# Chunk-wise norm behind the delta recurrence, leading parts first in the first tile, GpSimd held back, and sums of squares placed elsewhere, in a two-block network in one kernel

## The chip, the core and the metric

One core of a Trainium2 chip runs the whole program. The metric is the device time of one execution in microseconds (us). Engines are named as in the profile: PE is TensorE, PEld its weight loads, DVE VectorE, ACT ScalarE, POOL GpSimd, SP SyncE.

## The reference

512 tokens of width 1024, fp32. Two blocks follow each other. The first has a mixer of pooled means and a gated delta rule, then an MLP; the second has sparse attention and a state-space mixer. Here the first block matters, and of the second only its last product and norm.

```python
u = rms_norm(h, norm_mix[l])
proj = u @ w_in[l]                    # 20 tiles of 128 columns, and 8 columns a, b
...
def step(state, inp):                 # over chunks
    v_new = val - einsum(kc, state)
    o = einsum(qd, state) + einsum(ai, v_new)
    state = state * exp(gl) + einsum(kd, v_new)
...
o = o * lax.rsqrt(jnp.mean(o * o, axis=-1, keepdims=True) + EPS) * gdn_norm
o = o * jax.nn.silu(z)
...
h = h + mix @ w_out[l]                # mix: 512 pooled columns, then 4 heads of 128
u = rms_norm(h, norm_mlp[l])
h = h + jnp.square(jax.nn.relu(u @ w_up[l])) @ w_down[l]
```

## The kernel before

Activations lie transposed, 128 features per partition and 512 tokens along the row; hT holds x as eight such tiles (KT = 8). There is no scheduler: each engine has a list of instructions written out by hand, and they wait for each other by counting semaphores, so the order in the code is the order on the engine.

Each matrix product is made of three products of parts: a value is split into a leading part (suffix H, made by a rounding copy) and a rest (suffix L, the difference), and `product` (L396 to L398) adds leading x leading, rest x leading and leading x rest of one 128-row slice. The weights stream through a ring of four places (RING). One "half" is 128x512, four slices of one tile of outputs; two halves make a tile, so 24 products. SP loads half n into raw, POOL splits it (`split_weights`: a guard L1445, the cast L1446 into wh, the subtraction L1448 into wl; half_split counts), PE uses it (`half_slot`; half_used counts). A place of the ring is split again only when its half is used. Tiles alternate over four PSUM banks, and tile n+4 waits until tile n is evicted.

*The start.* ACT makes the leading parts of x times the norm weight (`weigh_lead`, L989, counted by g_lead) and DVE the rests (`weigh_rest`, L1539, counted by g_split); x comes in four pieces of two tiles. PE's first tile (`inp_tile(0)`) waits slice by slice for g_split. ACT then squares the eight tiles, DVE adds the squares (`add_square`, L1549), and `sum_squares(0)` (L389) sums them over the partitions by a product with ones, behind the second tile. `root` (L994, L995) makes the inverse root from it, which DVE needs for its first eviction (`evict_inp`, L1583). Behind tile 3 come the products with w_ab, whose small split POOL does between halves 3 and 4.

*The recurrence.* Four chunks of 128 tokens (NCH). Per chunk PE computes k x state (L649), the output of the chunk before (`scan_out`, L639 and L641) and the update (L661); DVE makes v_new and the state. ACT copies each chunk's output into gdnO (L1151). When all four are there ACT squares per head (L1155), PE sums (L668), ACT computes the inverse roots of four heads by Ln and Exp (`inverse_roots`, L970 and L973, with a table load before each), and DVE multiplies per head (L1749, L1752) into xs; ACT takes the leading part (`lead`, L1011) and DVE the rest (`rest`, L1534). `linear_apart("out")` takes the first four slices (the pooled ones) of tiles 0 to 3 first, 48 products, and their second halves after them; the first of these waits for m_split 5 to 8.

*The tail.* `linear_apart("sout")` is followed by residual additions (L1559), squares, additions, `sum_squares(4)`, the root, eight multiplications (L2210) and four output transfers of two tiles each (L1430).

## Time and profile before

| | us |
|---|---|
| median of 3 runs | 1330.87 |
| the runs | 1328.6, 1330.87, 1333.95 |
| profiled execution, its own time | 1328.44 |
| its span | 1326.6 |
| busy PE / POOL / DVE / ACT | 1271.9 / 857.1 / 779.4 / 414.0 |

The profiled execution's time holds 1.8 us around the span. Busy is the sum of what an engine's instructions took; what remains of PE's span, 54.7 us, is waiting. The mean granted clock of TensorE is 0.989 of full speed.

### The profile page before, as it was taken

Reading aid. Unit: us, or ns where it says so; the run is one execution under the profiler, and the core shown is the slowest. Engines: PE = TensorE matmul, PEld = TensorE weight load, DVE = VectorE, ACT = ScalarE, POOL = GpSimd, SP = SyncE. Lnnn points to the kernel's source line nnn. Section 1 sums busy time; section 2 is a strip of 40 time slices with the busy share of each in tenths; the row PEclk is TensorE's granted clock in tenths of the full one; section 3 lists DMA queues with packets and bytes.
Section 4 is the critical chain, followed back from the end, with each engine's and each line's share of the span. In section 5 each row is a group of like instructions: output and inputs, shape, how many; then the busy total and the mean of one; then the engine's idle time right before and its main releaser. Section 6 shows DMA issues by size and latency. Waiting matters only on the chain.

```text
span 1326.6 us, 21957 instructions
## 1 busy us (share of the span) xinstructions
PE 1271.9 (96%) x7696; PEld 1001.4 (75%) x7696; DVE 779.4 (59%) x1102; ACT 414.0 (31%) x850; POOL 857.1 (65%) x1078
## 2 busy tenths in 40 slices
PE   6999999899999999999999999899999999999995
PEld 4778897778877788888788798555557787878884
DVE  5968664689799211499438226277774659832223
ACT  4165744243301133211210021467773300331111
POOL 7767632777999777899778727312115875467772
PEclk9999999999999999999999999899999999999998
DMA  5222100253325433255495212100004459623331
GB/s 196 80 80 80 49 4 16 80 141 95 95 80 198 138 117 95 87 154 163 111 320 158 72 48 82 46 1 1 1 1 176 142 143 269 208 72 96 95 95 71
DMA packets 86476, 137.89 MB, mean 104 GB/s; under 512 B 16512, under 2 KB 34432, under 8 KB 85376
## 3 DMA queue, kind: packets, MB, share of 16 engines
q1 hardware_dynamic: 48384, 88.10, 22.2%
q10 hardware_dynamic: 38016, 48.71, 11.6%
q8 instruction: 55, 0.90, 0.3%
q14 instruction: 21, 0.17, 0.0%
HBM read 119.02 MB, written 20.91 MB: 105 GB/s over the span
## 4 chain that ended last, share of the span: by engine, by line
PE 82%; DVE 7%; issue 4%; POOL 3%; ACT 2%; DMA 1%; ACTq 1%; POOLq 0%; DVEq 0%
PE ps L396 20%; PE ps L398 20%; PE ps L397 20%; PE ps L811 3%; PE ps L791 3%; PE ps L835 3%; PE ps L549 2%; POOL small L1445 2%; DVE acc L1549 1%; PE ps L695 1%; PE ps L740 1%; PE ps L899 1%; POOL wh L1446 1%; PE ps L539 1%; DVE uL L1539 1%
## 5 line engine op out<-in xcount | busy, mean ns | idle before, releaser
L1448 POOL TENSOR_TENSOR wl<-raw,wh 128x512 fp32r<-128x512 f32 x336 | 498.6, 1484 | 26.9
L1445 POOL TENSOR_TENSOR small<-small 1x1 f32<-1x1 f32 x336 | 122.4, 364 | 261.8 <-PE ps L398 256.1
L396 PE MATMUL ps<-uH,wh 128*128 128x512 f32 x672 | 266.1, 396 | 11.1 <-DVE uL L1539 11.1
L397 PE MATMUL ps<-uL,wh 128*128 128x512 f32 x672 | 262.5, 391 | 0.0
L398 PE MATMUL ps<-uH,wl 128*128 128x512 f32 x672 | 262.3, 390 | 0.0
L1446 POOL CAST wh<-raw 128x512 fp32r<-128x512 f32 x336 | 203.3, 605 | 0.0
L396 PEld LDWEIGHTS ps<-uH,wh 128*128 128x128 f32 x672 | 126.6, 188 | 40.2 <-issue 11.0
L397 PEld LDWEIGHTS ps<-uL,wh 128*128 128x128 f32 x672 | 126.8, 189 | 27.2 <-issue 1.4
L398 PEld LDWEIGHTS ps<-uH,wl 128*128 128x128 f32 x672 | 126.7, 189 | 26.5
L396 PE MATMUL ps<-ffH,wh 128*128 128x512 f32 x256 | 101.4, 396 | 4.3 <-POOL wl L1448 4.3
L397 PE MATMUL ps<-ffL,wh 128*128 128x512 f32 x256 | 99.8, 390 | 0.0
L398 PE MATMUL ps<-ffH,wl 128*128 128x512 f32 x256 | 99.7, 390 | 0.0
L1511 POOL TENSOR_TENSOR bigA<-small 128x512 f32<-128x512 f32 x16 | 16.6, 1040 | 128.5 <-PE ps L844 100.0
L1313 ACT ACTIVATE bigB<-bigB,small 128x512 f32<-128x512 f32 (+3 forms) x128 | 70.3, 551 | 31.8 <-DVE small L2037 31.8
L2037 DVE CUSTOM_DVE_ANT_0 bigB<-ps,bigB 128x512 f32<-128x512 f32 (+3 forms) x128 | 57.3, 486 | 38.6 <-issue 23.5
L1559 DVE TENSOR_TENSOR hT<-hT,ps 128x512 f32<-128x512 f32 x40 | 27.5, 687 | 68.8 <-PE ps L398 68.3
L396 PEld LDWEIGHTS ps<-ffH,wh 128*128 128x128 f32 x256 | 48.0, 188 | 18.1 <-POOL wl L1448 6.1
L1889 DVE TENSOR_TENSOR ffL<-bigB,ffH 128x512 f32 x16 | 11.5, 719 | 79.4 <-ACT ffH L1231 79.4
L811 PEld LDWEIGHTS ps<-const_table,bigB 128*128 128x128 f32 x320 | 33.9, 141 | 31.9 <-issue 22.2
L1549 DVE TENSOR_TENSOR acc<-acc,xs 128x512 f32<-128x512 f32 x42 | 55.8, 1341 | 1.1 <-ACT xs L986 0.5
L398 PEld LDWEIGHTS ps<-ffH,wl 128*128 128x128 f32 x256 | 48.0, 188 | 10.2
L397 PEld LDWEIGHTS ps<-ffL,wh 128*128 128x128 f32 x256 | 48.1, 188 | 9.6
(395 smaller groups left out, 2395.0 us busy)
## 6 DMA issues: line engine op xcount, KB each, us to landing
raw<-wstream SPq DMA_DIRECT2D x336, 256.0 KB, 2.6
b_powers_scratch<-bigB ACTq DMA_DIRECT2D x4, 1024.0 KB, 5.1
c_powers_scratch<-bigB ACTq DMA_DIRECT2D x8, 512.0 KB, 4.1
lags_scratch<-lag_rows_scratch ACTq DMA_DIRECT2D x8, 512.0 KB, 8.4
bigB<-b_powers_scratch ACTq DMA_DIRECT2D x4, 1024.0 KB, 9.2
bigB<-lags_scratch ACTq DMA_DIRECT2D x4, 1024.0 KB, 6.6
bigB<-c_powers_scratch ACTq DMA_DIRECT2D x4, 1024.0 KB, 10.0
hT<-x ACTq DMA_DIRECT2D x4, 512.0 KB, 7.3
```

The costliest lines, as they stand in the source:

```text
L396: pe.matmul(out, lh, rh, start=first, stop=False)
L397: pe.matmul(out, lh, rl, start=False, stop=False)
L398: return pe.matmul(out, ll, rh, start=False, stop=last)
L791: i = pe.matmul(ps[:, u % 2 * 2 + half, 0:W], nsT[P, t, qt * 128:(qt + 1) * 128], nsT[P, 12 + 2 * b + t // 4, 0:W], start=True, stop=True)
L811: i = pe.transpose(ps[:, 4 + at // 512, at % 512:at % 512 + 128], prob[:, u % 6, half, kt * 128:(kt + 1) * 128], ident)
L835: i = pe.matmul(ps[64 * half:64 * half + 64, 7, kt * 128:512], vtok[:, kt, b * 256 + h * DH:b * 256 + (h + 1) * DH], probT[g % 2][:, half, ...
L1313: i = act.activation(prob[:, n % 6, half, 0:W], prob[:, n % 6, half, 0:W], ACT.Exp, scale=-1.0, bias=anmax[:, n % 3, half:half + 1], accum ...
L1445: pool.tensor_tensor(small[0:1, 569 + j:570 + j], zero_ap[0:1], zero_ap[0:1], ALU.add)
L1446: pool.tensor_copy(wh[:, j, :], raw[:, j, :]).then_inc(half_lead, 1)
L1448: pool.tensor_tensor(wl[:, j, :], raw[:, j, :], wh[:, j, :].bitcast(f32), ALU.subtract).then_inc(half_split, 1)
L1549: dve.tensor_tensor(acc[:, i, :], acc[:, i, :], xs[:, i if n == 2 else k % 2, :], ALU.add).then_inc(sq_added, 1)
L2037: i = dve.tensor_tensor_reduce(prob[:, u % 6, half, 0:W], ps[:, u % 2 * 2 + half, 0:W], dsl[t % 2][:, half, 512 - W:512], -1.0, 3e38, ALU. ...
```

## The change

It has these parts.

- **First tile** (`first_tile`): all 16 products that need only leading parts of x come first, two per slice as the part is ready, then the eight with the rests.
- **GpSimd held**: before it splits half 2 it waits for the sixth rest (`rests=KT - 2`); the second four halves now come ahead of w_ab. Before half 4 of "out" it waits for x_full, DVE's last step of the norm.
- **First sum** behind the third tile. ACT loads the table of Ln at its start.
- **Delta norm by chunks**: after each chunk's copy comes its square; the sum of chunk 0 stands within chunk 2, those of chunks 1 and 2 behind the recurrence, that of chunk 3 behind the first slice of "out". ACT makes the root of chunk 0 between chunks 1 and 2. DVE multiplies by chunks, in place; ACT makes four leading parts, DVE four rests.
- **Tail**: the last sum is two products, one of the first seven squares added up, one of the eighth. The output goes in five transfers.

```diff
@@ -189,6 +189,7 @@
+        go_bank = [4, 6, 5, 7]
@@ -355,7 +356,7 @@
-        SQUARES = [KT - 1, 2 * (KT - 1), 4 * (KT - 1), 5 * (KT - 1), 6 * (KT - 1)]
+        SQUARES = [KT - 1, 2 * (KT - 1), 4 * (KT - 1), 5 * (KT - 1), 6 * (KT - 1) - 1]
@@ -366,6 +367,12 @@
+        def go_squares(c):
+            return urr[1][:, c, :]
...
+        def of_chunk(x, c):
+            return x[:, 0:NHG, c * CH:(c + 1) * CH]
@@ -397,7 +404,7 @@
-            def half_slot(out, n, j, right, first, last, ready=None):
+            def half_slot(out, n, j, right, first, last, ready=None, between=None):
@@ -405,6 +412,8 @@
+                    if k == 0 and between is not None:
+                        between()
@@ -424,14 +433,14 @@
-            def linear_apart(name, x, ready):
+            def linear_apart(name, x, ready, between=None):
...
-                              h == 0, h == 1, (ready, 4 * h) if t == 0 else None)
+                              h == 0, h == 1, (ready, 4 * h) if t == 0 else None, between if i == 0 else None)
@@ -440,14 +449,29 @@
-                              lambda k: (uH[:, h * 4 + k, :], uL[:, h * 4 + k, :]), h == 0, h == 1,
-                              (g_split, 4 * h) if n == 0 else None)
...
-            inp_tile(0)
+                              lambda k: (uH[:, h * 4 + k, :], uL[:, h * 4 + k, :]), h == 0, h == 1)
...
+            def first_tile():
...
+                for h in range(2):
+                    pe.wait_ge(half_split, h + 1)
+                    for k in range(4):
+                        pe.wait_ge(g_lead, 4 * h + k + 1)
+                        for n, w in enumerate((wh, wl)):
+                            pe.matmul(ps[:, 0, :], w[:, h, k * 128:(k + 1) * 128], uH[:, h * 4 + k, :],
+                                      start=h == k == n == 0, stop=False)
+                for h in range(2):
+                    for k in range(4):
+                        pe.wait_ge(g_split, 4 * h + k + 1)
+                        i = pe.matmul(ps[:, 0, :], wh[:, h, k * 128:(k + 1) * 128], uL[:, h * 4 + k, :],
+                                      start=False, stop=h == 1 and k == 3)
+                    i.then_inc(half_used, 1)
...
+            first_tile()
...
+            inp_tile(2)
...
-            inp_tile(2)
@@ -641,6 +665,11 @@
+            def scan_squares(c):
...
+                pe.wait_ge(go_sq, c + 1)
+                pe.matmul(ps[:, go_bank[c], :], ones, go_squares(c), start=True, stop=True).then_inc(go_sum, 1)
@@ -649,6 +678,8 @@
+                    if c == 2:
+                        scan_squares(0)
@@ -662,13 +693,10 @@
-            for h in range(NHG):
-                pe.wait_ge(go_sq, h + 1)
-                pe.matmul(ps[:, 4 + h, :], ones, urr[1].rearrange("p a b -> p (a b)")[:, h * T:(h + 1) * T],
-                          start=True, stop=True).then_inc(go_sum, 1)
+            for c in range(1, NCH - 1):
+                scan_squares(c)
...
-            linear_apart("out", (mH, mL), m_split)
+            linear_apart("out", (mH, mL), m_split, between=lambda: scan_squares(NCH - 1))
@@ -942,7 +970,10 @@
-            sum_squares(4)
+            pe.wait_ge(sq_added, SQUARES[4])
+            pe.matmul(ps[:, 4, :], ones, acc[:, 0, :], start=True, stop=False)
+            pe.wait_ge(sq_done, SQUARED[4] + KT)
+            pe.matmul(ps[:, 4, :], ones, xs[:, (KT - 1) % 2, :], start=False, stop=True).then_inc(rms_sum, 1)
@@ -961,6 +992,7 @@
+            act.preload_act_table_set("natural_log")
@@ -1145,18 +1177,23 @@
+            def scan_roots(chunks):
+                inverse_roots(chunks, lambda c: of_chunk(qkvT, c), lambda c: ps[:, go_bank[c], :].rearrange("p (h c) -> p h c", c=CH),
+                              1.0 / 128, lambda c: act.wait_ge(go_sum, c + 1), go_std)
...
-                act.activation(gdnO[:, :, c * CH:(c + 1) * CH], src, ACT.Copy).then_inc(sc_oe, 1)
-            act.wait_ge(sc_oe, NCH)
-            sq = urr[1].rearrange("p a b -> p (a b)")
+                act.activation(of_chunk(gdnO, c), src, ACT.Copy).then_inc(sc_oe, 1)
+                act.wait_ge(sc_oe, c + 1)
+                act.activation(go_squares(c).rearrange("p (h c) -> p h c", c=CH), of_chunk(gdnO, c), ACT.Square).then_inc(go_sq, 1)
+                if c == 1:
+                    scan_roots(range(0, 1))
+            scan_roots(range(1, NCH))
+            act.wait_ge(x_full, NHG)
...
-                act.activation(sq[:, h * T:(h + 1) * T], gdnO[:, h, :], ACT.Square).then_inc(go_sq, 1)
-            inverse_roots(range(NHG), lambda h: qkvT[:, h, :], lambda h: ps[:, 4 + h, :], 1.0 / 128,
-                          lambda h: act.wait_ge(go_sum, h + 1), go_std)
-            for h in range(NHG):
-                lead(mH[:, 4 + h, :])
+                act.activation(mH[:, 4 + h, :], gdnO[:, h, :], ACT.Copy).then_inc(x_lead, 1)
+            full[0] = NHG
@@ -1425,19 +1462,22 @@
-            for k in range(0, KT, 2):
-                act.wait_ge(rms_out, k + 2)
-                act.dma_start(out_dram[:, k:k + 2, :], hT[:, k:k + 2, :]).then_inc(out_done, 16)
-            act.wait_ge(out_done, KT // 2 * 16)
+            parts = ((0, 2), (2, 4), (4, 6), (6, 7), (7, 8))
+            for lo, hi in parts:
+                act.wait_ge(rms_out, hi)
+                act.dma_start(out_dram[:, lo:hi, :], hT[:, lo:hi, :]).then_inc(out_done, 16)
+            act.wait_ge(out_done, len(parts) * 16)
...
-            def split_weights(lo, hi):
+            def split_weights(lo, hi, rests=None):
...
+                        if rests is not None and j == 2:
+                            pool.wait_ge(g_split, rests)
@@ -1461,9 +1501,10 @@
-            split_weights(0, RING)
+            split_weights(0, RING, rests=KT - 2)
+            split_weights(RING, 2 * RING)
...
-            split_weights(RING, 2 * SLOT0["out"] + RING)
+            split_weights(2 * RING, 2 * SLOT0["out"] + RING)
@@ -1486,6 +1527,7 @@
+            pool.wait_ge(x_full, NHG)
@@ -1742,19 +1784,18 @@
-            dve.wait_ge(sc_o, NCH)
...
+            for c in range(NCH):
+                dve.wait_ge(go_std, c + 1)
+                own(dve.scalar_tensor_tensor(of_chunk(gdnO, c), of_chunk(gdnO, c), param("gdn_norm"), of_chunk(qkvT, c), ALU.mult, ALU.mult))
+                i = dve.tensor_tensor(of_chunk(gdnO, c), of_chunk(gdnO, c), projT[:, 16:20, PAD + c * CH:PAD + (c + 1) * CH], ALU.mult)
+            i.then_inc(x_full, NHG)
+            dve.wait_ge(m_split, 4)
...
-                dve.wait_ge(go_std, h + 1)
-                own(dve.scalar_tensor_tensor(gdnO[:, h, :], gdnO[:, h, :], param("gdn_norm"), qkvT[:, h, :], ALU.mult, ALU.mult))
-                if h >= 2:
-                    dve.wait_ge(m_split, 4 + h - 1)
-                dve.tensor_tensor(xs[:, h % 2, :], gdnO[:, h, :], projT[:, 16 + h, PAD:PW], ALU.mult).then_inc(x_full, 1)
-                if h >= 1:
-                    if h == 1:
-                        dve.wait_ge(m_split, 4)
-                    rest(mL[:, 3 + h, :], mH[:, 3 + h, :]).then_inc(m_split, 1)
-            rest(mL[:, 7, :], mH[:, 7, :]).then_inc(m_split, 1)
+                dve.wait_ge(x_lead, h + 1)
+                dve.tensor_tensor(mL[:, 4 + h, :], gdnO[:, h, :], mH[:, 4 + h, :].bitcast(f32), ALU.subtract).then_inc(m_split, 1)
+            split[0] = NHG
@@ -2203,7 +2244,12 @@
-            residual("sout", 4, lambda k: add_square(4, k) if k else None)
+            for k in range(KT - 1):
+                add_tile("sout", k)
+                if k > 1:
+                    add_square(4, k - 1)
+            add_square(4, KT - 2)
+            add_tile("sout", KT - 1)
```

The start, on PE: the first rows before (names: uH and uL are leading part and rest of x, wh and wl those of the weights).

```order
L396 MATMUL ps<-uH,wh 128x512 [waits weighted_split,half_split]
L397 MATMUL ps<-uL,wh 128x512
L398 MATMUL ps<-uH,wl 128x512
L396 MATMUL ps<-uH,wh 128x512 [waits weighted_split]
L397 MATMUL ps<-uL,wh 128x512
L398 MATMUL ps<-uH,wl 128x512
```

And with the change, the first rows and those around the end of the first tile's leading products:

```order
L461 MATMUL ps<-uH,wh 128x512 [waits weighted_lead,half_split]
L461 MATMUL ps<-uH,wl 128x512
L461 MATMUL ps<-uH,wh 128x512 [waits weighted_lead]
L461 MATMUL ps<-uH,wl 128x512
...
L461 MATMUL ps<-uH,wh 128x512 [waits weighted_lead]
L461 MATMUL ps<-uH,wl 128x512
L466 MATMUL ps<-uL,wh 128x512 [waits weighted_split] x8
L403 MATMUL ps<-uH,wh 128x512 [waits half_split]
L404 MATMUL ps<-uL,wh 128x512
```

Each slice's product with uL has gone behind the 16 others. On POOL, around half 2, with the change:

```order
L1485 TENSOR_TENSOR small<-small 1x1 [waits half1_loaded]
L1486 CAST wh<-raw 128x512
L1488 TENSOR_TENSOR wl<-raw,wh 128x512 [waits half_lead]
L1485 TENSOR_TENSOR small<-small 1x1 [waits weighted_split,half2_loaded]
L1486 CAST wh<-raw 128x512
L1488 TENSOR_TENSOR wl<-raw,wh 128x512 [waits half_lead]
```

The guard of half 2 waits for weighted_split (g_split). On PE, between the end of the recurrence and "out", before (uT is the squares, mH and mL the mixed activations):

```order
L639 MATMUL ps<-bigA,mixT 128x128
L641 MATMUL ps<-bigB,mixT 128x128
L668 MATMUL ps<-uT,const_table 128x512 [waits gdn_squares] x4
L396 MATMUL ps<-mH,wh 128x512 [waits half_split,mixed_split,tile_evicted,scan_state]
L397 MATMUL ps<-mL,wh 128x512
L398 MATMUL ps<-mH,wl 128x512
L396 MATMUL ps<-mH,wh 128x512 [waits mixed_split]
L397 MATMUL ps<-mL,wh 128x512
L398 MATMUL ps<-mH,wl 128x512
```

With the change:

```order
L663 MATMUL ps<-bigA,mixT 128x128
L665 MATMUL ps<-bigB,mixT 128x128
L671 MATMUL ps<-uT,const_table 128x512 [waits gdn_squares] x2
L403 MATMUL ps<-mH,wh 128x512 [waits half_split,mixed_split,tile_evicted,scan_state]
L404 MATMUL ps<-mL,wh 128x512
L405 MATMUL ps<-mH,wl 128x512
L671 MATMUL ps<-uT,const_table 128x512 [waits gdn_squares]
L403 MATMUL ps<-mH,wh 128x512 [waits mixed_split]
L404 MATMUL ps<-mL,wh 128x512
L405 MATMUL ps<-mH,wl 128x512
L403 MATMUL ps<-mH,wh 128x512 [waits mixed_split]
```

Of the four sums two stand there and one behind the first three products; the fourth is earlier. On ACT, from the first copy of a chunk, before:

```order
L1151 ACTIVATE uT<-ps 128x4x128 [waits scan_out] x4
L1155 ACTIVATE uT<-uT 128x512 [waits scan_out_copied]
L1155 ACTIVATE uT<-uT 128x512 x3
L970 ACT_TABLE_LOAD
L970 ACTIVATE bigA<-ps,small 128x512 [waits gdn_sum] x4
L973 ACT_TABLE_LOAD
L973 ACTIVATE bigA<-bigA 128x512 [waits act_chain]
L973 ACTIVATE bigA<-bigA 128x512 x3
L1011 ACTIVATE mH<-xs 128x512 [waits x_full] x4
```

With the change:

```order
L1187 ACTIVATE uT<-ps 128x4x128 [waits scan_out]
L1189 ACTIVATE uT<-uT 128x512 [waits scan_out_copied]
L1187 ACTIVATE uT<-ps 128x4x128 [waits scan_out]
L1189 ACTIVATE uT<-uT 128x512 [waits scan_out_copied]
L1002 ACT_TABLE_LOAD
L1002 ACTIVATE bigA<-ps,small 128x4x128 [waits gdn_sum]
L1005 ACT_TABLE_LOAD
L1005 ACTIVATE bigA<-bigA 128x4x128 [waits act_chain]
L1187 ACTIVATE uT<-ps 128x4x128 [waits scan_out]
L1189 ACTIVATE uT<-uT 128x512 [waits scan_out_copied]
L1187 ACTIVATE uT<-ps 128x4x128 [waits scan_out]
L1189 ACTIVATE uT<-uT 128x512 [waits scan_out_copied]
```

Squares follow the copies, and two table loads have come in between the second and the third chunk.

## Rows read from the trace of the kernel before

**Rows 1.** The page, busy time and share of the span by engine.

```profile
PE 1271.9 (96%) x7696; PEld 1001.4 (75%) x7696; DVE 779.4 (59%) x1102; ACT 414.0 (31%) x850; POOL 857.1 (65%) x1078
```

**Rows 2.** Timeline, start to 31 us: start us, length, engine line what [idle<-releaser].

```profile
6.15 1.28 ACT L989 ACT_TABLE_LOAD   x1 [6.15 <-DMA hT<-x]
...
8.20 8.46 DVE L1539 SCALAR_TENSOR_TENSOR uL<-hT,param_table,uH 128x512 fp32r<-128x512 f32 x8 [3.38 <-ACT uH L989]
...
9.56 0.76 PE L396 MATMUL ps<-uH,wh 128*128 128x512 f32 x1 [9.56 <-DVE uL L1539]
...
11.61 1.33 ACT L989 ACTIVATE uH<-hT,param_table 128x512 fp32r<-128x512 f32 x2 [0.31 <-DMA hT<-x]
...
14.58 0.63 PE L397 MATMUL ps<-uL,wh 128*128 128x512 f32 x1
...
15.01 0.43 PE L398 MATMUL ps<-uH,wl 128*128 128x512 f32 x1
...
21.76 0.64 POOL L1445 TENSOR_TENSOR small<-small 1x1 f32<-1x1 f32 x1
...
23.26 0.39 PE L398 MATMUL ps<-uH,wl 128*128 128x512 f32 x1
...
24.58 0.64 POOL L1445 TENSOR_TENSOR small<-small 1x1 f32<-1x1 f32 x1
...
26.46 1.10 PE L389 MATMUL ps<-acc,const_table 128*128 128x512 f32 x2 [2.82 <-DVE acc L1549]
...
30.94 0.63 ACT L995 ACTIVATE rms<-rms 128x512 f32<-128x512 f32 x1
```

**Rows 3.** Timelines, 215 to 241 us; a window: engines' busy time, granted clock last but two.

```profile
215.09 0.60 ACT L1151 ACTIVATE uT<-ps 128x512 f32<-128x512 f32 x1 [1.19 <-PE ps L641]
...
216.40 3.70 PE L668 MATMUL ps<-uT,const_table 128*128 128x512 f32 x8 [1.35 <-ACT uT L1155]
...
217.92 1.28 ACT L970 ACT_TABLE_LOAD   x1
...
219.22 2.43 ACT L970 ACTIVATE bigA<-ps,small 128x512 f32<-128x512 f32 x4
...
222.93 0.18 POOL L1445 TENSOR_TENSOR small<-small 1x1 f32<-1x1 f32 x1 [25.87 <-PE ps L398]
...
229.07 1.22 DVE L1534 TENSOR_TENSOR mL<-xs,mH 128x512 fp32r<-128x512 f32 x1
...
233.06 1.75 DVE L1534 TENSOR_TENSOR mL<-xs,mH 128x512 fp32r<-128x512 f32 x1
...
219.53 0.80 PE L396 MATMUL ps<-mH,wh 128*128 128x512 f32 x1
...
234.87 0.50 PE L396 MATMUL ps<-mH,wh 128*128 128x512 f32 x1 [3.19 <-DVE mL L1534]
...
240.38 0.40 PE L398 MATMUL ps<-mH,wl 128*128 128x512 f32 x1
...
236.80:240.40 3.60, 3.54 (x9) 2.78 (x10) 1.33 (x3) 0.07 (x1) 0.58 (x2) 0.53 0.02 5
```

**Rows 4.** Timelines of ScalarE and VectorE, tail; window with DMA share last but one.

```profile
1313.18 1.28 ACT L994 ACT_TABLE_LOAD   x1
1315.47 0.69 ACT L994 ACTIVATE rms<-ps,small 128x512 f32<-128x512 f32 x1 [1.01 <-PE ps L389]
...
1313.56 0.69 DVE L1549 TENSOR_TENSOR acc<-acc,xs 128x512 f32<-128x512 f32 x1 [0.46 <-ACT xs L986]
...
1323.00:1325.00 2.00, 0.00 (x0) 0.00 (x0) 0.53 (x1) 0.00 (x0) 0.00 (x0) 0.50 0.99 395
```

**Rows 5.** VectorE's first rests, 0 to 20 us: count, min/median/max ns.

```profile
L1539 DVE SCALAR_TENSOR_TENSOR uL<-hT,param_table,uH x8: 740/1010/1772, 8.2 to 15.8; 128x512 fp32r<-128x512 f32 x8
```

**Rows 6.** Timeline of VectorE near 75 us.

```profile
75.29 0.69 DVE L1583 TENSOR_TENSOR bigA<-ps,rms 128x512 f32<-128x512 f32 x1 [4.52 <-PE ps L398]
```

**Rows 7.** Waits of TensorE, 355 to 436 us: total, times, longest us.

```profile
PE ps L396 <- POOL wl L1448: 4.3, 5, 1.0
```

## The prediction

> **What bounds the kernel now.** I read the page first: TensorE is busy 96% of the span [rows 1], so only time in which it waits, or runs at its lower clock, can be won. The table of what TensorE waited for, narrowed to each stage, gives the places, and the order of instructions in time shows them one by one. Three of them lie where the change works.
>
> - *The start.* The first product is at 9.56, though a split weight half is there much earlier. It waits for VectorE's first rest (uL), which waits for ScalarE's first leading part, which waits for a table load that only begins when x has landed. Then the first tile's products come at a pace of 0.43 us each until 15.01, and at 0.229 us from there on (36 products from 15.01 to 23.26). From 23.49 to 26.46 TensorE stands before the first sum of squares, because VectorE's eight rests and seven additions are not through [rows 2].
> - *The end of the chunk recurrence.* ScalarE copies the last chunk at 215.09, squares four heads, TensorE sums them from 216.40, ScalarE changes tables twice, VectorE multiplies. TensorE covers this with 48 products of "out" and then stands still, 3.19 us at 234.87; the tile that waits is finished at 240.61 (its last product starts at 240.38) [rows 3].
> - *The tail.* Last addition, sum, root, output: nothing runs beside it [rows 4].
>
> VectorE is slow beside GpSimd when its inputs lie in SBUF: the eight first rests take 0.74 to 1.77 us [rows 5], two rests of "out" 1.22 and 1.75 [rows 3], while an addition at 1313.56, with GpSimd idle, takes 0.69 [rows 4]. That is what "GpSimd held back" buys.
>
> **The start, step by step.** All times are in the clock of the old trace. The table is loaded before x lands, so leading part 1 is ready at 6.15 + 0.70 = 6.9 instead of 8.2. The first tile now runs its 16 products that need only leading parts, two per part. ScalarE makes the parts at 0.64 us each; the last two wait for the fourth piece of x at 11.61 [rows 2] and end at 12.95, so the table load saves nothing there. The 16 products end at 12.95 + 2 x 0.43 = 13.8. VectorE's rests, 0.74 us each with GpSimd idle [rows 5], keep step: the sixth at about 11.9, the eighth at 13.7. Eight products are left: 1.8 us at the faster pace. It came 5.4 us after the first product before; the same here would be 12.3, so I take it. The tile ends at 15.6; before, at 18.05 (the second tile's 24 products end at 23.49). If the pace is still the slow one it is 8 x 0.43 = 3.4, and 17.2.
>
> GpSimd's hold goes on until the sixth rest, 11.9. Its steps per half (guard, cast, subtraction) took 24.58 - 21.76 = 2.82 us beside VectorE [rows 2]; so halves 2 to 7 end at 14.7, 17.6, 20.4, 23.2, 26.0 and 28.8. TensorE wants halves 2 to 5 at 15.6, 18.3, 21.1 and 23.8, and after the sum (0.94) halves 6 and 7 at 27.5 and 30.2. The smallest margin is 0.6 us, so the hold costs nothing; if it lasts 1 us longer it costs 0.4. The small split of w_ab, now behind half 7, ends at 30, and is wanted at 33. The sum of squares stands behind the third tile at 26.5; the additions end before 24, so the wait of 2.97 us goes. **Gain: 2.45 + 2.97 = 5.4 us**, 5.2 with a trifle for GpSimd's margin; bounds 3.4 (the slow pace, 3.8, and a hold 1 us longer) and 6.0 (the last piece of x 0.6 us sooner). What is late next: the inverse root, ready at 31.57 before, comes at about 30.3 (sum at 26.5, no table load before Ln), and VectorE then works off a backlog without a pause until 70.8. Its first wait for TensorE after that, up to 75.29, was 4.52 us [rows 6], so with 1.3 us from the earlier root it can follow a shift of 5.8. That just covers 5.2.
>
> **The recurrence.** TensorE gets the same four sums (0.86 us each, four in 3.70 us at 216.40 [rows 3]) at other places. The first goes into chunk 2 ahead of the output of chunk 1 and delays what follows by 0.86, as VectorE was already done there. The outputs of the last chunk end at 215.7 instead of 214.9. ScalarE now makes a copy and a square of 0.6 us per chunk, and between chunks 1 and 2 the root of chunk 0: two table loads of 1.28 us [rows 3] and two activations, from 211.2 to 215.1. So the last copy and square, one behind the other with chunk 2's, end at 217.5, against 217.9 for four squares. Sums 1 and 2 are done at 217.5, "out" begins there (219.53 before) and takes sum 3 in behind its third product; its first 48 products end at 229.3. ScalarE: load to 218.8, three Ln, the last after sum 3, to 220.6, load, Exp at 222.5, 223.1 and 223.6. VectorE: two steps per chunk of 0.74 + 0.69 us, since GpSimd is held, so x_full at 222.5 + 3 x 1.45 = 226.8. Before, most of the same steps ran beside GpSimd's splitting. Then four leading parts at 0.55 to 0.63 us and four rests; GpSimd starts its splits at 226.8 too (222.93 before [rows 3]), so the rests take between 0.7 and 1.75 us; I take 1.4, from the two measured there, 1.22 and 1.75 [rows 3]. They end at 229.1, 230.5, 231.9 and 233.3. Half 4 of the weights is split at 229.4. The waiting tile ends at 233.3 + 0.7 = 234.0; before, 240.61. The later halves, one per 2.82 us from 229.4, stay ahead of TensorE, which wants them at 234.0, 236.7 and 239.4 (half 7 by 237.9). **Gain 6.6 us.** Bounds: 8.3 with rests of 0.7 us, 5.0 with the clock below. I take 6.2.
>
> The load of a table shows as 1.28 us, and the Ln behind it starts at once, at 219.22, so I price each of the two added loads at that [rows 3].
>
> **The tail.** The last square ends at 1313.17, the last addition starts 0.39 us later, takes 0.69, and the sum starts at 1314.31. Now the sum of the first seven squares is taken at once behind the last tile, and the last square is its own second product, from 1313.2 to 1314.3. The Ln then starts at 1314.5, as its table load ends at 1314.46 [rows 4]: 1.0 us before the old 1315.47. The last output is issued in smaller pieces, but the transfer engines are 99% busy from 1323 to 1325 [rows 4], so this gives 0 to 0.4; I take 0. **Gain 1.0 us**, bounds 0.8 and 1.4.
>
> **The sum**: 5.2 + 6.2 + 1.0 = 12.4 us. From the profiled execution's 1328.44 that is 1316.0; the median of the runs shown is 2.4 us above that execution, so I forecast **1318.5 us**. Between the three places TensorE is the chain nearly everywhere, and waits for work that itself follows TensorE, so the gains should be carried to the end.
>
> **Rivals.**
> *The clock takes a share back.* In the window from 236.8 to 240.4 the granted clock is 0.53, the lower level but for its end, and nine products take 3.6 us, after TensorE had waited twice [rows 3]. The new kernel waits there as well, between single groups of three products, about 2.5 us in all, and in the first tile its products come in pairs with gaps. If the clock is at 1.2 GHz through the first tile's last eight products (1.6 us) and again through eight of "out" (1.6 us), the gain is 9.2: 1321.7. For it: that window. Against it: the new waits are shorter. The page "TensorE: Matmul & The Clock Gate" of the Trainium skill, What's actually happening, says that the array is at half rate by default and that activity releases it; the trace agrees, with the slow pace up to 15.01. Chance 0.2.
> *A change of tables costs more than its load.* The detour to chunk 0's root holds ScalarE from 211.2 to 215.1, and each us longer comes one for one out of "out". If each of the two loads in it cost as much again as it shows, 2.6 us, the time is 1321.1. Against it: the step from the load at 217.92 to the next activation is 1.30 us [rows 3]. Chance 0.05. The Trainium skill, "ScalarE: Activation LUTs", What ACT_TABLE_LOAD costs, says so: a drain of about 1.38 us comes with every load, 2.66 us in all. By that page the detour is 2.8 us longer and the sum 9.6; the trace shows no such drain.
> *The start's gain is lost on the way.* Stretches that hang on GpSimd exist: around the first "up" and "down" TensorE waited five times for a split, 4.3 us [rows 7]. If such a stretch, or VectorE's backlog before 70.8, doesn't move forward with TensorE, the 5.2 is gone and 1323.7 remains. For it: VectorE's margin is only 0.6 us. Against it: in every one of these stretches GpSimd itself begins on TensorE's release. Chance 0.12.
> *The holds make GpSimd the bound: slower.* Both holds delay the splits, and TensorE pays one for one beyond its margin: 0.6 us at the start, 0 to 4 in "out". It turns the result from where the two holds together last 13 us longer than I have them (the 12.4 and the margin); at 15.6 us, the loss is 15 against the forecast: 1333.5. For it: before the change the eight rests lasted until 16.66. Against it: they did so beside GpSimd. Chance 0.03.
> *It doesn't do what it says*: the rests stay slow with GpSimd idle, or x's pieces land later. Then the start gives 3 and "out" 3, and 1323.9 results. Chance 0.05.
> The forecast's own case has 0.55.
>
> **How the numbers follow.** About 0.5%, 6.7 us, is what a measurement of this kernel can tell from no change. The forecast, the clock rival and the table rival, 0.8 together, lie beyond it; of the other two, 7.2 and 7.0 us are just beyond, so I count half of their 0.17 as faster, and take off a little for the spread of the runs (5.35 us between three of them): faster 0.85, same 0.12, slower 0.03. Range: upper bounds of all terms, 6.0 + 8.3 + 1.4 = 15.7, and 2.3 us of spread give 1313; the lost start, with 1.8 us of spread, gives 1325.5.
>
> **What would show it.** Right: first product near 7; first tile done by 16; no wait before the first sum; rests of 0.75 us there; "out" beginning near 217.5 less the shift of 5, its waiting tile done 6 to 7 us earlier relative to the last recurrence step; Ln of the tail 1.0 us sooner. Wrong: a TensorE wait for wl of halves 2 to 7 or 4 of "out", the low clock in the first tile or behind the waits of "out", or VectorE idle no more near 75 and TensorE waiting for its small gate step (L494).

## The result, and the profile after

| | before | changed |
|---|---|---|
| median, us | 1331.01 (4 runs, 1328.6 to 1333.95) | 1321.64 (4 runs, 1321.18 to 1323.33) |
| ratio | | 0.9927, 95% interval 0.9914 to 0.994 |
| profiled execution, its own time | 1328.44 | 1323.33 |
| its span | 1326.6 | 1321.5 |

The change is 9.4 us faster: the side that was forecast, 3.1 us short of the forecast time of 1318.5, inside the range. The two profiled executions differ by only 5.1 us. Before's was the fastest of its runs and the changed kernel's the slowest, so where the time went is read from places, not from the spans. Of all runs told of below, one took 1609.95 us (x5, granted clock 0.747); the ratios leave it out.

**A ruler.** GpSimd makes one subtraction (wl) for each of the 336 weight halves, in the same order in every version. The start of the n-th in a trace, taken from the start of the n-th in the trace of before, says by how much a version is ahead at that place. Halves are counted from 0. Hereafter "lead at half n" is that difference, positive when the version is ahead. For the changed kernel:

```
half   12    20    24    28    40  |  60    188 |  192   232 |  244   300 | end of the span
lead   5.3   5.0   2.4   1.9   1.9 |  7.7   7.8 |  6.1   6.0 |  4.2   4.2 | 5.1
```

It makes 5 us at the start, loses 3 between halves 20 and 28, makes 5.9 at the recurrence, loses 1.7 and 1.8 in two stretches at the lower clock in the middle (3.4 us long from 651.8, where before has none, and 17.1 us long from 849.8, where before has 13.7), and makes 0.9 at the tail.

The page, busy time by engine, answers to [rows 1]: TensorE has 3.8 us more busy time in a span 5.1 us shorter. Busy time holds the products at the lower clock, so it is no measure of work.

```profile
PE 1275.7 (97%) x7698; PEld 1002.5 (76%) x7698; DVE 773.1 (59%) x1101; ACT 415.7 (31%) x851; POOL 856.8 (65%) x1078
```

**The start**, the timeline of the changed kernel to 31 us, by engine (start us, length, engine, line, what, idle time before and who ended it), answers to [rows 2]:

```profile
4.82 1.28 ACT L995 ACT_TABLE_LOAD   x1 [4.82 <-issue]
...
8.16 1.34 ACT L1021 ACTIVATE uH<-hT,param_table 128x512 fp32r<-128x512 f32 x2 [0.70 <-DMA hT<-x]
...
6.99 0.77 PE L461 MATMUL ps<-uH,wh 128*128 128x512 f32 x1 [6.99 <-ACT uH L1021]
7.55 0.63 PE L461 MATMUL ps<-uH,wl 128*128 128x512 f32 x1
7.98 0.63 PE L461 MATMUL ps<-uH,wh 128*128 128x512 f32 x1
...
9.96 0.47 PE L461 MATMUL ps<-uH,wh 128*128 128x512 f32 x1
10.27 0.40 PE L461 MATMUL ps<-uH,wl 128*128 128x512 f32 x1
...
13.68 2.28 PE L466 MATMUL ps<-uL,wh 128*128 128x512 f32 x8
15.80 0.39 PE L403 MATMUL ps<-uH,wh 128*128 128x512 f32 x1
...
26.71 1.02 PE L396 MATMUL ps<-acc,const_table 128*128 128x512 f32 x2
...
6.88 3.81 DVE L1581 SCALAR_TENSOR_TENSOR uL<-hT,param_table,uH 128x512 fp32r<-128x512 f32 x4 [2.09 <-ACT uH L1021]
...
12.47 2.93 DVE L1581 SCALAR_TENSOR_TENSOR uL<-hT,param_table,uH 128x512 fp32r<-128x512 f32 x2 [0.20 <-ACT uH L1021]
...
30.64 0.69 DVE L1625 TENSOR_TENSOR bigA<-ps,rms 128x512 f32<-128x512 f32 x1 [5.53 <-PE ps L405]
...
12.43 0.18 POOL L1485 TENSOR_TENSOR small<-small 1x1 f32<-1x1 f32 x1 [4.28 <-DVE uL L1581]
```

The first product is at 6.99 (9.56 before). ScalarE makes the leading parts as x lands, and waits for it three times, at 8.16 for 0.70 us. TensorE reaches its faster pace at about 9.96: the step to the next product is 0.31 us there, against 0.43 from 7.55 to 7.98. Seven of the eight rest products follow each other at 0.23 us, the eighth starts at 15.46, when its rest is there; the tile ends at 15.80, and the first sum, at 26.71, has no idle time ahead of it. VectorE's rests, merged in these rows, take 1.82 us for the first, beside GpSimd's split of half 1, 0.74 to 0.75 for each of the next five, with GpSimd held, and 1.23 and 1.78 for the last two, once GpSimd is released at 12.43.

**The gate step**, the same view from 62 to 78 us, VectorE, ScalarE and TensorE:

```profile
63.56 0.68 DVE L1625 TENSOR_TENSOR bigA<-ps,rms 128x512 f32<-128x512 f32 x1
...
69.21 2.81 DVE L1658 SCALAR_TENSOR_TENSOR bigA<-bigA,param_table 128x512 f32<-128x512 f32 x3 [2.14 <-ACT bigA L1064]
71.95 0.68 DVE L1625 TENSOR_TENSOR bigA<-ps,rms 128x512 f32<-128x512 f32 x1
...
77.23 0.18 DVE L1687 SCALAR_TENSOR_TENSOR small<-small 128x16 f32<-128x16 f32 x1
...
63.67 0.22 ACT L1086 ACTIVATE small<-small 128x16 f32<-128x16 f32 x1 [5.29 <-DVE small L1677]
...
68.47 0.71 ACT L1064 ACTIVATE bigA<-bigA,param_table 128x512 f32<-128x512 f32 x1
...
75.25 0.39 PE L405 MATMUL ps<-uH,wl 128*128 128x512 f32 x1
77.46 0.39 PE L518 MATMUL ps<-small,const_table 128*128 128x16 f32 x2 [1.82 <-DVE small L1687]
```

VectorE takes 32.9 us from its first eviction (30.64) to that of tile 6 (63.56); before, it took 30.3 (31.76 to 62.03). Here are the two rows of before that answer to 63.56 and 69.21, with the first product behind the recurrence's waiting tile, which is needed further down:

```profile
239.53 0.63 PE L396 MATMUL ps<-mH,wh 128*128 128x512 f32 x1
...
62.03 0.68 DVE L1583 TENSOR_TENSOR bigA<-ps,rms 128x512 f32<-128x512 f32 x1
...
67.68 3.09 DVE L1616 SCALAR_TENSOR_TENSOR bigA<-bigA,param_table 128x512 f32<-128x512 f32 x3 [0.38 <-ACT bigA L1032]
```

So tile 6's eviction comes 1.5 us later than before, though everything up to there began 1.1 us earlier. A chain hangs on VectorE's step right before that eviction (L1677): four activations of ScalarE from 63.67, with three table loads between them, then its scaling at 68.47, then VectorE's next block at 69.21, which is 1.5 us later than before too. VectorE's work then ends at 71.95, where before it ended at 70.77 and stood idle for 4.52 [rows 6]. The gate step (L1687) is ready at 77.41, and TensorE, whose last product started at 75.25, waits 1.82 us for it. Then the clock falls. Windows of TensorE there (length, busy time, granted clock, DMA share, GB/s):

```profile
78.00:80.00 2.00, 2.00 (x7) 0.60 0.24 86
80.00:82.00 2.00, 2.00 (x7) 0.55 0.30 103
```

**The recurrence**, timeline from 205 to 233 us, answers to [rows 3]:

```profile
215.17 0.80 PE L403 MATMUL ps<-mH,wh 128*128 128x512 f32 x1
...
227.86 0.50 PE L403 MATMUL ps<-mH,wh 128*128 128x512 f32 x1 [0.36 <-POOL wl L1488]
...
231.25 0.50 PE L403 MATMUL ps<-mH,wh 128*128 128x512 f32 x1 [0.72 <-DVE mL L1796]
...
209.38 1.28 ACT L1002 ACT_TABLE_LOAD   x1
210.68 0.69 ACT L1002 ACTIVATE bigA<-ps,small 128x512 f32<-128x512 f32 x1
...
215.62 1.28 ACT L1002 ACT_TABLE_LOAD   x1
216.91 1.85 ACT L1002 ACTIVATE bigA<-ps,small 128x512 f32<-128x512 f32 x3
...
224.37 0.69 DVE L1791 TENSOR_TENSOR uT<-uT,bigA 128x512 f32<-128x512 f32 x1
225.83 5.36 DVE L1796 TENSOR_TENSOR mL<-uT,mH 128x512 fp32r<-128x512 f32 x4 [0.77 <-ACT mH L1195]
...
225.38 0.18 POOL L1485 TENSOR_TENSOR small<-small 1x1 f32<-1x1 f32 x1 [30.20 <-DVE uT L1791]
```

The root of chunk 0 lies between the chunks (209.38 to 213.31), "out" begins at 215.17, x_full is done at 225.06, the four rests take 1.34 us each, and the waiting tile is finished at 232.05. Where TensorE had waited 3.19 and 1.03 us and run at 0.53 of the clock [rows 3], it now waits 0.36 (for GpSimd's split of half 4 of "out", which the hold delays) and 0.72, and the clock stays at 1.00.

**The tail**, timeline, answers to [rows 4]:

```profile
1309.06 1.13 PE L976 MATMUL ps<-xs,const_table 128*128 128x512 f32 x2 [0.58 <-ACT xs L1018]
...
1308.38 0.63 ACT L1018 ACTIVATE xs<-hT 128x512 f32<-128x512 f32 x1 [4.81 <-DVE hT L1601]
1309.03 1.28 ACT L1026 ACT_TABLE_LOAD   x1
1310.32 0.69 ACT L1026 ACTIVATE rms<-ps,small 128x512 f32<-128x512 f32 x1
```

The product of the last square ends at 1310.19, ScalarE's table load at 1310.31, and Ln starts at once. From the start of the last square to the end of the span: 1308.38 to 1321.5, 13.1 us, against 14.07 before (1312.53 to 1326.6).

### The profile page after: what moved, and what is told of

It is laid out like the page before. It is cut to its first block, busy times and chain, and to the rows that moved or that the text cites. A ratio compares the mean times of both kernels' runs of the same rounds, so it can differ in the third digit from the quotient of the medians.

```text
span 1321.5 us, 21957 instructions
## 1 busy us (share of the span) xinstructions
PE 1275.7 (97%) x7698; PEld 1002.5 (76%) x7698; DVE 773.1 (59%) x1101; ACT 415.7 (31%) x851; POOL 856.8 (65%) x1078
## 4 chain that ended last, share of the span: by engine, by line
PE 80%; DVE 8%; issue 4%; POOL 3%; ACT 2%; DMA 1%; ACTq 1%; POOLq 0%; DVEq 0%
PE ps L403 20%; PE ps L404 19%; PE ps L405 19%; PE ps L839 3%; PE ps L819 3%; PE ps L863 3%; PE ps L573 2%; POOL small L1485 2%; PE ps L723 1%; PE ps L768 1%; PE ps L927 1%; POOL wh L1486 1%; PE ps L563 1%; DVE bigB L1632 1%; DVE bigA L2096 1%
## 5 line engine op out<-in xcount | busy, mean ns | idle before, releaser
L1485 POOL TENSOR_TENSOR small<-small 1x1 f32<-1x1 f32 x336 | 125.2, 373 | 258.1 <-PE ps L405 217.5
L403 PE MATMUL ps<-uH,wh 128*128 128x512 f32 x664 | 262.8, 396 | 1.5 <-DVE uL L1581 1.5
L404 PE MATMUL ps<-uL,wh 128*128 128x512 f32 x664 | 259.2, 390 | 0.0
L405 PE MATMUL ps<-uH,wl 128*128 128x512 f32 x664 | 259.2, 390 | 0.0
L1930 DVE TENSOR_TENSOR ffL<-bigB,ffH 128x512 f32 x16 | 11.1, 692 | 79.9 <-ACT ffH L1268 79.9
L819 PE MATMUL ps<-bigA 64*128 64x512 f32 (+3 forms) x256 | 54.8, 508 | 1.1 <-ACT bigB L1331 0.7
## 6 DMA issues: line engine op xcount, KB each, us to landing
bigB<-c_powers_scratch ACTq DMA_DIRECT2D x4, 1024.0 KB, 10.1
```

The source lines that it names most:

```text
L403: pe.matmul(out, lh, rh, start=first, stop=False)
L404: pe.matmul(out, lh, rl, start=False, stop=False)
L405: return pe.matmul(out, ll, rh, start=False, stop=last)
L819: i = pe.matmul(ps[:, u % 2 * 2 + half, 0:W], nsT[P, t, qt * 128:(qt + 1) * 128], nsT[P, 12 + 2 * b + t // 4, 0:W], start=True, stop=True)
L1485: pool.tensor_tensor(small[0:1, 569 + j:570 + j], zero_ap[0:1], zero_ap[0:1], ALU.add)
```

## The experiments

Twelve kernels. Medians beside the runs of before on the same chip (median 1331.1 of 19 runs for the first four, 1331.7 of 27 for the next, 1330.8 of 21 for the last). The change was measured beside its own four runs of before, so a difference of under 1 us between its median and another's is no finding. Leads are from each one's trace, one per kernel, by the ruler above.

| | median us | ratio, 95% | lead 12 | lead 20 | lead 28 | lead 60 | made at "out" |
|---|---|---|---|---|---|---|---|
| the change | 1321.6 | 0.991-0.994 | 5.3 | 5.0 | 1.9 | 7.7 | 5.86 |
| x1 start only | 1326.5 | 0.996-1.000 | 4.9 | 4.7 | 3.2 | 2.7 | |
| x2 recurrence only | 1322.9 | 0.992-0.996 | -1.8 | -1.7 | -1.7 | 4.1 | 5.84 |
| x3 tail only | 1330.3 | 0.998-1.000 | -2.2 | -1.7 | -1.7 | -2.0 | |
| x4 late gate | 1317.9 | 0.988-0.992 | 4.9 | 4.7 | 5.3 | 11.1 | 5.86 |
| x5 first sum late only | 1328.5 | 0.997-1.000 | 3.0 | 2.6 | 2.4 | 1.9 | |
| x6 no hold at "out" | 1325.2 | 0.994-0.998 | 4.8 | 4.7 | 3.1 | 5.7 | 2.54 |
| x7 no hold at the start | 1322.6 | 0.991-0.995 | 0.8 | 0.5 | 0.9 | 6.8 | 5.88 |
| x8 roots together | 1321.8 | 0.991-0.995 | 4.9 | 4.7 | 1.5 | 5.7 | 4.12 |
| x9 late gate, old start | 1331.3 | 0.999-1.001 | -2.0 | -1.6 | -1.1 | -1.7 | |
| x10 no early table load | 1322.2 | 0.990-0.994 | 3.8 | 3.6 | 0.4 | 6.3 | 5.87 |
| x11 tail, sum only | 1330.7 | 0.998-1.002 | -1.9 | -1.9 | -1.8 | -1.7 | |
| x12 late gate again | 1316.9 | 0.988-0.991 | 5.0 | 4.8 | 5.3 | 11.2 | 5.88 |

**One group of parts at a time** (x1 to x3). The edits are the parts of the change named in the section on it; x1 has `first_tile`, the late first sum, the early table load and the hold at the start; x2 the norm by chunks and the hold at "out"; x3 the last sum in two products and the five transfers.

```diff
-            inp_tile(0)
+            first_tile()
...
+            act.preload_act_table_set("natural_log")
...
+            split_weights(0, RING, rests=KT - 2)
```

> The start's parts alone in the old kernel (first tile's order, first hold of GpSimd, w_ab behind half 7, first sum behind the third tile, table of Ln at the start). Theory A (the gain is made and then lost to VectorE's backlog): the splits of halves 12 to 20 are 5.3 us earlier than in the old kernel, TensorE waits about 1.8 us at its small gate products near 77 us, then works through about ten products at the lower clock, and from half 28 on the lead is 1.9 us; the time is 1.9 us lower than before (1329), unclear within the noise. Rival B (the loss of 3.4 us comes from the other parts or was chance of one execution): no such wait and a time 5.3 us lower, 1325.7.

Lead 4.9 at half 12, 3.2 at half 28: 1.5 to 1.8 us are lost at the gate step, where TensorE waits 1.82 us as in the changed kernel. The clock did not fall behind that wait here, which is the rest of the difference to the changed kernel's 1.9. The median, 1326.5, is 2.5 us below theory A's 1329 and nearer to rival B's 1325.7. Theory A holds in the trace all the same, wait and loss are there; its 1.9 us were a lead over a trace of before that is faster than the usual one (see x2), and counted in a fall of the clock that didn't come.

```diff
+            for c in range(1, NCH - 1):
+                scan_squares(c)
...
+            linear_apart("out", (mH, mL), m_split, between=lambda: scan_squares(NCH - 1))
...
+            pool.wait_ge(x_full, NHG)
```

> The parts of the recurrence alone in the old kernel (norm by chunks, sums placed elsewhere, GpSimd held until x_full). Theory A: the chain through out's waiting tile is its own, so the splits from half 64 on are 5.9 us earlier than before and the time is 5.9 us lower, 1325. Rival B (it only gains because the start came earlier): under 3 us.

5.84 us made at "out". The lead is -1.7 up to there although nothing ahead of it was changed: with the old start, TensorE stands 2.37 us before the first sum and then runs at the lower clock. So does x3, so do x9 and x11 (3.2 to 3.3 us); only the trace of before doesn't, after 2.82 us. Before's profiled execution is a lucky one by 1.7 us. The median is 8.2 us below before's, where 5.9 was expected; the interval goes from 5.7 to 10.1. A part of the surplus is in the trace: its low stretch near 850 is 10.2 us long, 3.4 shorter than before's, and the lead grows there from 4.2 to 5.4.

```diff
-            sum_squares(4)
+            pe.wait_ge(sq_added, SQUARES[4])
+            pe.matmul(ps[:, 4, :], ones, acc[:, 0, :], start=True, stop=False)
...
+            parts = ((0, 2), (2, 4), (4, 6), (6, 7), (7, 8))
```

> The last sum in two products and five output transfers alone in the old kernel. Theory A: from the last square's start to the end 13.1 us instead of 14.1, time 1.0 us lower, within the noise of the runs; all of it before the Ln, none in the transfers. Rival B (smaller last transfers also end sooner): 1.3 us or more, and the end 2.7 us or less behind the last multiplication, 3.1 before.

Last square to the end 1314.83 to 1328.0, 13.2 us. The median is only 0.8 us below before, within what the runs can tell; the trace has it. The three medians add up to 13.7 us and the whole change made 9.4. With intervals as wide as x1's (0.4 to 5.6) and x2's, the runs don't tell whether the parts lose something together.

**The gate step moved** (x4), with the whole change in:

```diff
+            inp_tile(10)
             pe.wait_ge(gate_b, 2)
             pe.wait_ge(pool_out, 3)
             pe.matmul(ps[:, 6, 0:16], const("cumsum"), gg, start=True, stop=True)
             pe.matmul(ps[:, 6, 16:32], ones, gg, start=True, stop=True).then_inc(gate_mm, 1)
-            inp_tile(10)
```

> The changed kernel with TensorE's two small gate products (cumsum, sum of gg) moved from in front of tile 10 to behind it; VectorE reads them only after it has evicted tile 10. Theory A: TensorE no longer waits 1.8 us for VectorE's gate step there, does not fall to the lower clock behind it, and the lead over the old kernel stays 5.3 us from half 20 to half 40: time 3.4 us below the changed kernel, 1318.3. Rival B (VectorE is behind by then in any case and its next eviction or the sums of q and k wait instead): the wait shows up at the next place within 15 us and less than 1 us is won. Rival C (the clock falls at that place whatever TensorE waits for): 1.8 us is won and the low clock stays.

The windows of TensorE (columns as above) where the changed kernel had stood and then run at 0.60:

```profile
78.00:80.00 2.00, 2.00 (x10) 1.00 0.29 113
```

No wait, full clock, and the lead stays at 5.3 where the changed kernel falls to 1.9. One line moved is worth 3.4 us in the trace and about 4 in the medians.

**Is VectorE's backlog a fixed length?** (x5, from the kernel before)

```diff
             inp_tile(1)
-            pe.wait_ge(s_const, 16)
-            sum_squares(0)
             inp_tile(2)
+            pe.wait_ge(s_const, 16)
+            sum_squares(0)
```

> The kernel before with one edit: the product of the first sum of squares stands behind the third tile instead of behind the second. Theory A (VectorE's backlog from the root of that sum to the gate step is the second bound of the first 80 us): TensorE's wait ahead of the sum (2.4 to 3.3 us in the traces with the old start) goes and the clock stays high behind it, so the split of half 12 comes 3 us earlier than in the trace of before and 4.7 us earlier than in the two other traces with the old start; but the sum, and with it the root, comes 1 to 2 us later than at 30.94, so VectorE reaches the gate step 1 to 2 us later than before and TensorE waits there for 4 to 5 us: nothing is left of it by half 28, and the time is 1330 to 1332. Theory B (the lead is kept, and the wait at the gate step is small): half 28 and all after it 3 us or more earlier, time 1326.5 to 1328.5.

A miss for theory A as it was put. Timeline rows of TensorE at the gate step and of VectorE's evictions of tiles 0 and 6:

```profile
78.54 0.40 PE L494 MATMUL ps<-small,const_table 128*128 128x16 f32 x2 [0.97 <-DVE small L1645]
...
34.09 0.69 DVE L1583 TENSOR_TENSOR bigA<-ps,rms 128x512 f32<-128x512 f32 x1 [7.37 <-ACT rms L995]
...
62.97 0.68 DVE L1583 TENSOR_TENSOR bigA<-ps,rms 128x512 f32<-128x512 f32 x1
```

The root is 2.3 us later (33.90 against 31.57), but tile 6 is evicted only 0.9 us later: the stretch takes 28.9 us, where it took 30.3 before and 32.9 in the changed kernel. It isn't a fixed amount of work in time; VectorE's operations on SBUF take longer beside a GpSimd split (in the changed kernel the same multiplication, L1658, takes 0.74 to 1.65 us), and the earlier the stretch begins, the more splits not yet held up by TensorE lie beside it. The traces bear this out. Between the two evictions VectorE has the same 36 operations in all 14. GpSimd starts 8 subtractions (wl) there in x5, and the stretch takes 28.9 us; 9 in the kernel before, x2, x3, x7, x9 and x11, 29.8 to 30.8 us; 10 in x10, 31.6; 11 in the changed kernel, x1, x4, x6, x8 and x12, 32.9 to 33.0. That is about 1.3 us for a split more. No run changes the number of splits there by itself. TensorE's products of the gate step start at 78.54 here, at 77.77 in x1, 77.46 in the changed kernel and 78.94 in x10, although the roots of these lie up to 3.4 us apart. By itself this one edit keeps 2.4 of its 3 us by the ruler (more against the other traces with the old start, which lie at -1.7), and the time, 1328.5, is theory B's.

**The holds** (x6, x7).

```diff
-            pool.wait_ge(x_full, NHG)
```

> The changed kernel without GpSimd's wait for x_full ahead of the splits of the output projection's ring. Theory A (the hold buys short operations of VectorE, as taken in the prediction): the first split of that stretch starts at about 217 instead of 225.4, the multiplications of the last chunks take 0.8 to 1.3 us each instead of 0.69 to 0.75, x_full comes 1.5 to 3 us later than 225.06, the four remainders take 1.7 us each instead of 1.34, and the waiting tile ends 2.5 to 4.5 us later than at 232.05: time 1323.5 to 1326. Rival (the holds change nothing, since TensorE then waits for GpSimd instead): the tile ends within 0.5 us of 232.05 and the time is that of the changed kernel, 1321.6.

2.54 us made at "out" instead of 5.86: the hold is worth 3.3. The rows (VectorE's multiplications and rests, TensorE's wait):

```profile
225.65 1.58 DVE L1790 TENSOR_TENSOR uT<-uT,bigA 128x512 f32<-128x512 f32 x1
228.00 3.53 DVE L1795 TENSOR_TENSOR mL<-uT,mH 128x512 fp32r<-128x512 f32 x4 [0.77 <-ACT mH L1195]
...
229.87 0.47 PE L403 MATMUL ps<-mH,wh 128*128 128x512 f32 x1 [3.62 <-DVE mL L1795]
```

Five of the six multiplications take 1.2 to 1.7 us, more than the expected 0.8 to 1.3. Of the rests only the first takes 1.7 us; the other three take 0.68, not 1.7: GpSimd's fourth split ends at 229.2, the ring is full and GpSimd is quiet. x_full is ready at 227.24, and x6 is 1.2 us further ahead than the changed kernel up to there, so it is 3.4 us late, more than the 1.5 to 3 expected. TensorE stands 3.62 us, and the clock falls. The 3.3 us include what that fall costs.

```diff
-            split_weights(0, RING, rests=KT - 2)
+            split_weights(0, RING)
```

> The changed kernel without the hold at the start: GpSimd splits the third half as soon as it is there, beside VectorE's remainders. Theory A: the remainders take 1.2 to 1.8 us each instead of 0.94 to 1.46 and the last one ends at 16 to 17 instead of at 15.4, so the first tile ends 0.5 to 1.5 us later than at 15.80, and the splits from half 12 on come later by as much; since VectorE's backlog takes back what the start gains beyond the gate step anyway, the time stays within 0.7 us of 1321.6. Rival (the remainders are late because of the leading parts' arrival and not because of GpSimd): tile 0 ends at 15.8 as before, GpSimd is up to 4 us further ahead, and the stretch to the gate step is shorter, time 1320 to 1321.

```profile
7.25 11.02 DVE L1581 SCALAR_TENSOR_TENSOR uL<-hT,param_table,uH 128x512 fp32r<-128x512 f32 x8 [2.05 <-ACT uH L1021]
...
18.32 0.74 PE L466 MATMUL ps<-uL,wh 128*128 128x512 f32 x1 [1.17 <-DVE uL L1581]
18.87 0.63 PE L403 MATMUL ps<-uH,wh 128*128 128x512 f32 x1
```

The eight rests take 11.02 us, 1.38 each. TensorE waits 0.65 and 1.17 us within the first tile, which ends at 18.87, 3.1 us later than with the hold, more than theory A's 0.5 to 1.5, and the last rest ends at 18.27, where 16 to 17 was expected. The clock falls at 18.4 for 3.4 us, and the pace of 0.43 us follows. Lead 0.8 at half 12. Most of it doesn't matter, since at half 28 the changed kernel has only 1.9 left: 1.0 us in the trace and 0.9 in the medians, where at most 0.7 was expected.

**The root of chunk 0** (x8) and **the early table load** (x10), each taken out of the changed kernel:

```diff
-                if c == 1:
-                    scan_roots(range(0, 1))
-            scan_roots(range(1, NCH))
+            scan_roots(range(NCH))
```

> The changed kernel with the root of the first chunk not taken on its own but together with the other three: two table loads fewer on ScalarE, four chunks of logarithms and exponentials behind the last sum instead of three, and VectorE multiplies all four chunks behind it. Theory A (behind the last sum every operation on ScalarE and VectorE is on the path): the first exponential ends 0.6 us later and one more chunk of 1.4 us stands on VectorE, of which 0.3 to 0.7 us is given back since ScalarE's copy of chunk 2 no longer waits behind the root; x_full at 226.3 to 226.8 instead of 225.06, the waiting tile ends 1.2 to 1.7 us later, time 1322.8 to 1323.3. Rival (the two loads saved are worth as much as the chunk): x_full within 0.4 us of 225.06, time 1321.6.

```profile
220.70 2.20 ACT L1005 ACTIVATE bigA<-bigA 128x512 f32<-128x512 f32 x4
...
226.46 0.69 DVE L1789 TENSOR_TENSOR uT<-uT,bigA 128x512 f32<-128x512 f32 x1
...
229.93 0.80 PE L403 MATMUL ps<-mH,wh 128*128 128x512 f32 x1 [2.09 <-POOL wl L1486]
```

The exponentials end at 222.9 and x_full is ready at 227.15, 1.75 us later than in the changed kernel once its lead is the same (x8 is 0.34 us behind there). TensorE stands 2.09 us for GpSimd's split, which the hold ties to x_full, the clock falls behind that, and 4.12 instead of 5.86 us are made at "out". So two table loads more are the cheaper way in the trace, and the rival's "x_full within 0.4 us" is out. In the medians nothing of it shows: 1321.8 is the rival's time, 1 us below what was expected. Medians of 4 and of 10 runs that spread over several us don't resolve it, and x8's trace has a low stretch near 850 of 10.2 us, 6.8 shorter than the changed kernel's.

```diff
-            act.preload_act_table_set("natural_log")
```

> The changed kernel without the early load of the logarithm table. Theory A (the start's gain comes from the sum moved and from the order of the products, and the leading parts are paced by the arrival of x): the first leading part starts at 7.5 to 7.8 instead of at 6.12, the last one at most 0.5 us later than before (12.4), tile 0 ends 0 to 0.7 us later than at 15.80, and the table is loaded once before the first logarithm, at 28 to 30, which puts the root 1.3 us later; TensorE's wait at the gate step then grows by 0 to 1 us: time 1321.5 to 1322.8. Rival (each step of the start counts in full): tile 0 ends 1.3 us later and the time is 1323 to 1324.

A miss for theory A's steps, though the median, 1322.2, is in its range: the first tile ends at 17.34, 1.54 us later, and lead 28 is 0.4 against 1.9. The leading parts were nearly on time (the last at 13.5, against 13.06), but the first product comes at 8.90 instead of 6.99, and the pace stays at 0.43 us for 14 of the 16 products, against six in the changed kernel. What the early load buys here is an earlier start of TensorE's slow products, not earlier parts. How much of the 1.54 us that is, one trace doesn't tell. The faster pace came 6.1 us after the first product here. In the six traces with the new start and the hold (the change, x1, x4, x6, x8, x12) it came 3.0 to 5.3 us after it, and the tile ended at 15.62 to 16.16 wherever it came. Had it come 5.3 us after it here, products 13 to 24 would have run at 0.23 us and the tile ended near 16.9, 1.1 us late, by estimate from these rows; and after 4.3 us the tile would be 0.7 late.

**Two controls** (x9: x4's edit in the kernel before; x11: x3 with the four equal transfers) **and a repeat** (x12: x4 once more).

> The kernel before with one edit: the two products of the gate step stand behind the eleventh tile (tile 10) instead of behind tile 9. Theory A (at the gate step the old start leaves TensorE only 0 to 0.3 us early, so there is nothing to free): the wait of 0.25 us at those products goes, all splits behind half 24 stay within 0.4 us of the shift that they had at half 20, time that of before, 1331 to 1332. Rival (the gate products are better off later for another reason, by the order of the work on the other engines): 1 us or more faster than before.

Ratio 0.9998. In the lead, 0.5 us are won at the gate step (the wait of 0.25 and the products around it), 0.1 more than expected. What is worth 3.4 us behind the new start is worth next to nothing with the old one.

> The kernel before with the last sum of squares in two products (and the last addition on VectorE behind it), but with the four equal transfers at the end. Theory A (the sum carries all of the tail's gain, the last multiplication's end to the program's end was 3.08 us with four transfers and 3.13 with five): from the last square's start to the end 13.1 us, as in the changed kernel, against 14.07 before; time 1329.8 to 1330.7. Rival (the smaller last transfer carries half of it): 13.5 us or more from the last square to the end, time 1330.7 to 1331.2.

```profile
1315.77 0.63 ACT L989 ACTIVATE xs<-hT 128x512 f32<-128x512 f32 x1 [4.81 <-DVE hT L1562]
...
1317.71 0.69 ACT L997 ACTIVATE rms<-ps,small 128x512 f32<-128x512 f32 x1
```

Last square to the end of the span (1328.9): 13.1 us. The sum gives all of it, the fifth transfer nothing.

> The changed kernel with the gate step's products behind tile 10, a second time and in more runs, since its first median rests on four. Theory A (TensorE keeps the 5.3 us of the start instead of 1.9 to 3.2): splits 28 to 40 stand 5.0 to 5.5 us ahead of before, and the median lies 2 to 4 us below the changed kernel's 1321.6, at 1317.5 to 1319.5. Rival (the first result was a lucky set of runs, and the clock takes the lead back elsewhere): 1320 to 1322.

1316.9, ratio 0.9896. Over both, nine runs lie between 1316.1 and 1319.6, the changed kernel's four between 1321.2 and 1323.3. This version beats both kernels.

**Where the clock fell.** From short windows of granted clock over all 14 traces. A fall is to 0.50, the lower of the two levels:

| TensorE had stood | traces | clock fell behind it |
|---|---|---|
| 2.1 to 3.6 us at "out" | before, x1, x3, x5, x6, x8, x9, x11 | 8 of 8 |
| at most 0.72 us at "out" | the change, x2, x4, x7, x10, x12 | 0 of 6 |
| 2.4 to 3.3 us at the first sum | before, x2, x3, x9, x11 | 4 of 5 |
| 1.82 us at the gate step | the change, x1, x6, x8, x10 | 3 of 5 |
| 0.65 and 1.17 us in the first tile | x7 | 1 of 1 |
| 1.53 us near 650 | all | 3 of 14 (the change, x6, x10) |
| ten times 0.24 to 0.78 us within 15 us, shortly ahead of 850 | all | 14 of 14 |
| one or two waits of 0.8 to 1.3 us near 1110 | all | 1 of 14 (x9) |

A fall at the first sum, the gate step or near 650 lasts 3.4 us and costs 1.5 to 1.7 beyond the wait. The wait near 650 is for VectorE's rest of a norm, in every version; here are the first product behind it in the changed kernel, and a window with the low clock that came there and not before:

```profile
650.07 0.50 PE L403 MATMUL ps<-uH,wh 128*128 128x512 f32 x1 [1.53 <-DVE uL L1581]
...
652.00:655.00 3.00, 3.00 (x5) 0.50 0.23 75
```

The stretch near 850 is at the lower clock for 10.2 us in x2 and x8, 13.7 in before, x1, x3, x5, x9 and x12, and 17.1 in the change, x4, x6, x7, x10 and x11; x4 and x12 are the same kernel. x9 alone has a stretch at 792 to 806 too, with no wait over 0.51 us ahead of it, the same wait as in x3, whose clock stays at 1.00 there; it costs 6.3 us (its profiled span is 1336.5). So a part of why equal kernels differ by several us from run to run is which of these waits the clock falls behind, and for how long. What decides it stays open.

## Why the prediction came out as it did

- **The start as such: right.** First product at 6.99 (forecast near 7), tile 0 ended at 15.80 (15.6), root at 30.45 (30.3), no wait before the sum, no wait for a split weight half. 5.0 to 5.3 us against 5.2.
- **"That just covers 5.2": this step failed.** The prediction let VectorE's backlog move forward with the root (1.3 us) and added its idle 4.52 [rows 6]. The root did move, but the backlog grew by 2.65 us, since two more of GpSimd's splits lay in it. Instead of 4.52 + 1.3 = 5.8 only 4.52 - 1.2 = 3.3 us were there (VectorE through at 71.95 instead of 70.77): x1 and x6 keep 3.2 and 3.1. The changed kernel's trace keeps 1.9, because the clock fell behind the wait. x4 and x12 take the wait away and keep 5.3. The last of the prediction's own signs of being wrong, "TensorE waiting for its small gate step", is what came. The rival "the start's gain is lost on the way" (0.12) named this place and this mechanism, with the whole 5.2 as its price; 2 to 3.4 is what it was.
- **The early table load** was taken as worth nothing for the parts ("the table load saves nothing there"). The end of the parts was right, and without the load the tile still ended 1.5 us later (x10), through the start and the pace of the products; a part of that may be the late pace of that one trace. The pace was taken to change at 12.3 with the load in place; it did at 9.96 in the changed kernel and at 11.35 to 12.70 in x1, x4, x6, x8 and x12, with no effect on the end of the tile.
- **The recurrence: steps right, size off by a misread row.** "Out" began at 215.17 (217.5 less the lead of 1.9: 215.6), x_full was ready at 225.06 (224.9), the rests took 1.34 (1.4), the waiting tile ended at 232.05 (232.1). Gained were 5.9, not 6.6: the tile of before ended at 239.53, shown above. The prediction took the product group at 240.38 for its last, which is the first group of the next tile. In the new kernel that group takes another 0.7 us, and 240.61 - (234.0 + 0.7) is the 5.9 that was measured; the 6.2 taken in the sum was 0.3 too much. TensorE did wait for the split of half 4 of "out", one of the signs of being wrong, but for 0.36 us only.
- **The holds** do what was said of them: 3.3 us at "out" (x6), 3.1 at the first tile, of which 1.0 is kept (x7). With GpSimd held, the rests of the first tile took 0.74 to 0.75 us and the multiplications by chunks 0.69 to 0.75, as forecast.
- **The tail: right**, 0.95 us against 1.0, all from the sum (x11), none from the transfers.
- **The clock rival** (1321.7, chance 0.2) has the measured time but neither of its places: the first tile's last eight products and the whole of "out" ran at 1.00. The low clock fell behind the gate step, where no rival put it. So that its number fits is luck. What the change did was the reverse, to remove the low stretch at "out". The Trainium skill, "TensorE: Matmul & The Clock Gate", What's actually happening, has the array at half rate by default and activity releasing it; the table above agrees with that as far as long waits go, 12 falls behind 13 waits of over 2 us.
- **The table rival** did not come: a load takes 1.28 us and the activation behind it starts 1.29 to 1.30 us after it (209.38 to 210.68, 215.62 to 216.91). The detour to chunk 0's root took 3.9 us, as forecast. The Trainium skill, "ScalarE: Activation LUTs", What ACT_TABLE_LOAD costs, adds a drain to each load; no row shown here has one. By its figure of 1.38 us the detour would have taken 6.7, by estimate.
- **The base.** The prediction took the profiled execution of before for the kernel and added 2.4 us. The four traces with the same old start run 1.7 us later from half 8 on: the median's kernel has a low-clock stretch behind the first sum. The new start removes it, a gain that the prediction didn't have and that partly offset the losses at the gate step. That the forecast missed by 3.1 us and not by more is luck to that extent.

Summed by the ruler, against before's median kernel: 1.7 (clock at the first sum) + 1.9 to 3.2 (start, kept) + 5.9 + 1.0 = 10.5 to 11.8; 9.4 was measured, with an interval of 8.0 to 11.4. How often the low stretches near 650 and 850 come, and how long they are, is not in this sum.

## What to carry to other kernels

A gain on the bounding engine is kept only as far as the next small step that it waits for. For that step follow the other engine's own chain, with the durations that it will have at the new time, before you count its idle time as room; and when the gain is made, look for what has become early enough to be moved behind another block of work: here one moved line brought back 3.4 us. Compare two traces by the same n-th instruction of one engine instead of by their spans, and look whether the trace you started from is a typical one.

## What was not expected of the hardware

- How long VectorE's backlog takes depends on when it runs: the same 36 operations, first eviction to that of tile 6, took 28.9 us in x5, 30.3 before and 32.9 in the changed kernel, with 8, 9 and 11 of GpSimd's splits beside them.
- A wait of TensorE of over 2 us was followed by a stretch at the lower clock in 12 of 13 cases, one of 1.82 us in three of five, one of 1.53 us in 3 of 14, with the same wait each time. What decides between them stays open.
- Ten waits of under 0.8 us each, 3.6 us in all within 15, were followed by 10 to 17 us at the lower clock in every trace. No experiment here touched that place, nor those near 650 and 800.
